# The last two tiles' squares of four norms go to TensorE

## What is computed

```
def rmsnorm(x, g):
    xf = x.astype(jnp.float32)
    y = xf * lax.rsqrt(jnp.mean(xf * xf, axis=-1, keepdims=True) + EPS)
    return y.astype(x.dtype) * g
...
    x = x + gate1 * (merged @ w_out[l])
    h2 = _rmsnorm(x, norm2_g[l]) * (1.0 + scale2) + shift2
    x = x + gate2 * _conv_ffn(h2, w_up[l], conv_w[l], conv_b[l], w_down[l])
return _rmsnorm(x, final_g)
...
    h = rmsnorm(x, g_mix)
    proj = h @ w_in
...
    x = x + merged @ w_o
    h2 = rmsnorm(x, g_ffn)
    a, b = jnp.split(h2 @ w_up, 2, axis=-1)
```

## Time and profile before

| | us |
|---|---|
| median of 3 runs | 894.43 |
| lowest, highest | 894.06, 895.6 |
| span of the profiled execution | 894.5 |
| busy in it: TensorE matmuls, VectorE, ScalarE | 853.3, 594.6, 409.9 |
| adds of this kind (L717): 35 | 0.43 us each |
| matmuls of the means by this line (L1219): 20 passes | 0.17 to 0.38 us each |

### The profile page before, as it was taken

One profiled execution on the slowest core, in us unless ns is written; L12 is line 12 of the kernel. 1 busy time (PEld: TensorE's weight loads), 2 busy tenths in 40 slices (PEclk: granted clock), 3 DMA queues, 4 the chain that ended last, 5 costly groups with the idle time before them and its releaser, 6 DMA issues.

```text
span 894.5 us, 16350 instructions
## 1 busy us (share of the span) xinstructions
PE 853.3 (95%) x6912; PEld 839.3 (94%) x6912; DVE 594.6 (66%) x789; ACT 409.9 (46%) x516; POOL 6.1 (1%) x22
## 2 busy tenths in 40 slices
PE   3499999998999999999999999999999899999998
PEld 3499899998899999999999999999999899999998
DVE  5987899477976656656774348644586766656663
ACT  3344666433544444434653345555424654434440
POOL 1100000000000000000000000000000000000000
PEclk9999999999799999999999999999999799999999
DMA  9788468537465555553265335353544455455511
GB/s 355 316 326 331 144 209 318 191 132 282 193 232 188 185 177 173 178 182 140 96 236 174 110 141 189 105 180 141 188 143 175 152 181 178 174 181 184 188 47 48
DMA packets 23676, 166.85 MB, mean 187 GB/s; under 512 B 2752, under 2 KB 3008, under 8 KB 3520
## 3 DMA queue, kind: packets, MB, share of 16 engines
q1 hardware_dynamic: 23040, 164.64, 51.2%
q10 hardware_dynamic: 576, 1.35, 0.4%
HBM read 164.93 MB, written 1.05 MB: 186 GB/s over the span
## 4 chain that ended last, share of the span: by engine, by line
PE 90%; DVE 6%; DMA 2%; issue 1%; ACT 0%; SPq 0%; DVEq 0%; ACTq 0%
PE ps L1167 78%; PE ps L1207 6%; DMA raw<-in_w_ada 2%; PE ps L1258 1%; PE ps L1245 1%; PE ps L1316 1%; DVE ada L674 1%; DVE wlo L689 1%; PE ps L1228 1%; DVE ada L678 1%; PE ps L1345 1%; PE ps L1297 1%; PE ps L1296 1%; DVE probs L828 0%; DVE tmp L754 0%
## 5 line engine op out<-in xcount | busy, mean ns | idle before, releaser
L689 DVE TENSOR_TENSOR wlo<-raw,whi 128x2048 fp32r<-128x2048 f32 x131 | 299.4, 2290 | 187.9 <-ACT whi L364 187.4
L1167 PE MATMUL ps<-hhi,whi 128*128 128x256 f32 x1368 | 392.2, 287 | 0.0
L1167 PE MATMUL ps<-hlo,whi 128*128 128x256 f32 x1368 | 387.9, 284 | 0.0
L1167 PE MATMUL ps<-hhi,wlo 128*128 128x256 f32 x1368 | 387.8, 283 | 0.0
L364 ACT ACTIVATE whi<-raw 128x2048 fp32r<-128x2048 f32 x131 | 249.9, 1910 | 176.2 <-PE ps L1167 149.6
L1167 PEld LDWEIGHTS ps<-hhi,whi 128*128 128x128 f32 x1368 | 263.1, 192 | 4.6 <-issue 4.5
L1167 PEld LDWEIGHTS ps<-hlo,whi 128*128 128x128 f32 x1368 | 263.2, 192 | 0.1
L1167 PEld LDWEIGHTS ps<-hhi,wlo 128*128 128x128 f32 x1368 | 263.0, 192 | 0.0
L1167 PE MATMUL ps<-fhi,whi 128*128 128x256 f32 x352 | 99.8, 284 | 0.3 <-DVE flo L1024 0.3
L1167 PE MATMUL ps<-fhi,wlo 128*128 128x256 f32 x352 | 99.7, 283 | 0.0
L1167 PE MATMUL ps<-flo,whi 128*128 128x256 f32 x352 | 99.7, 283 | 0.0
(11 more groups left out here) (163 smaller groups left out, 951.5 us busy)
## 6 DMA issues: line engine op xcount, KB each, us to landing
raw<-in_w_up SPq DMA_DIRECT2D x44, 1024.0 KB, 4.9
raw<-in_w_in SPq DMA_DIRECT2D x43, 1024.0 KB, 4.9
raw<-in_w_ada SPq DMA_DIRECT2D x24, 1024.0 KB, 6.2
raw<-in_w_down SPq DMA_DIRECT2D x22, 1024.0 KB, 4.9
raw<-in_branches SPq DMA_DIRECT2D x10, 1024.0 KB, 5.1
raw<-in_w_out SPq DMA_DIRECT2D x4, 1024.0 KB, 4.8
raw<-in_w_mem_kv SPq DMA_DIRECT2D x4, 1024.0 KB, 4.8
raw<-in_w_o SPq DMA_DIRECT2D x4, 1024.0 KB, 4.8
```

The costliest lines, as they stand in the source:

```text
L689: V.tensor_tensor(wlo[:, w % SPLIT, :], raw[:, r % RAW, :], f32(whi[:, w % SPLIT, :]), ALU.subtract).then_inc(raw_done, 1)
L1167: ins = mm(out_, l, r, start=start and i == 0, stop=stop and i == 2, **kw)
```

## The change

VectorE adds tiles 0 to 5 only in "two", "final", "mix" and "ffn2" (five adds instead of seven; "mem" stays as it is). TensorE's mean then has six matmuls instead of two: tile 0, which now holds the sum of tiles 0 to 5, and tiles 6 and 7 straight from ScalarE's squares, all accumulated in the same two columns of PSUM. Ahead of tile 6 TensorE waits for the norm's fourth pair of squares: `sq_ready` counts 4 for each norm, and NORM_SQUARES says how many norms came before.

```diff
--- before.py
+++ after.py
@@ -116,6 +116,7 @@
     STAT[_name] = (N_STAT, NT * (_tiles * _heads or 1))
     N_STAT += STAT[_name][1]
 SUMMED = ("mem", "two", "final", "mix", "ffn2")
+NORM_SQUARES = {"two": 2, "final": 3, "mix": 4, "ffn2": 5}
 BCAST = 256
 
 
@@ -715,7 +716,7 @@
                 for c in (2 * i, 2 * i + 1):
                     if c:
                         ins = V.tensor_tensor(src[:, 0, :], src[:, 0, :], src[:, c, :], ALU.add)
-                        if c < KT - 1:
+                        if c < (KT if name == "mem" else KT - 2) - 1:
                             link(ins)
                         else:
                             ins.then_inc(sem(f"{name}_summed"), 1)
@@ -980,7 +981,6 @@
                     sum_squares("two", 2, mg, u - 1)
                 if u in (1, 2):
                     split_low(w + AHEAD)
-            sum_squares("two", 2, mg, 3)
             norm_wide(1, "two", x, lambda c: gs2[:, c:c + 1], shift=mod[:, 24:32])
             split_low(WO1 + 3 + AHEAD)
 
@@ -1062,7 +1062,7 @@
                     ins = V.scalar_tensor_tensor(out=x[:, c, :], in0=ps[:, 4 + u, S * i:S * i + S],
                                                  scalar=mod[:, 40 + c:41 + c], in1=x[:, c, :], op0=ALU.mult, op1=ALU.add)
                 ins.then_inc(sem("x2_ready"), 1)
-            for i in range(4):
+            for i in range(3):
                 sum_squares("final", 3, mg, i)
             split_low(MEMKV + 3)
             invert("final")
@@ -1145,7 +1145,6 @@
                     sum_squares("ffn2", 5, mg, u - 1)
                 if u in (1, 2):
                     split_low(w + AHEAD)
-            sum_squares("ffn2", 5, mg, 3)
             norm_wide(4, "ffn2", x, lambda c: col("g_ffn_2", c))
             split_low(WO2 + 3 + AHEAD)
             ffn(1)
@@ -1214,9 +1213,14 @@
                 tiles, heads, bank, _ = NORMS[name]
                 mean = mean_64[:, 0:P:64] if heads == 2 else (mean_128 if heads else mean_d)[:, 0:1]
                 if name in SUMMED:
+                    parts = (0,) if name == "mem" else (0, KT - 2, KT - 1)
                     pe.wait_ge(sem(f"{name}_summed"), 1)
-                    for tt in range(NT):
-                        ins = mm(ps[:, bank, tt:tt + 1], src[:, 0, P * tt:P * tt + P], mean, start=True, stop=True)
+                    for c in parts:
+                        if c == KT - 2:
+                            pe.wait_ge(sem("sq_ready"), 4 * NORM_SQUARES[name] + 4)
+                        for tt in range(NT):
+                            ins = mm(ps[:, bank, tt:tt + 1], src[:, c, P * tt:P * tt + P], mean,
+                                     start=c == 0 and tt == 0, stop=c == parts[-1], skip_group_check=True)
                     ins.then_inc(sem(f"{name}_mean"), 1)
                     return
                 for c in range(tiles):
```

## The result

The changed kernel is slower: 899.34 us median of 5 runs (lowest 897.77) against 894.43 us; by the ratio, 1.0044 with an interval of 1.003 to 1.0057, it is +3.9 us. One of the five executions took 1052.92 us at a mean granted clock of 0.751: the ratio leaves it out, the median doesn't, and the other four have a median of 898.74 us. The forecast was 896.3 us, with a range to 898.0: the sign was right, the size too small. Its profiled execution has a span of 897.4 us and a time of 899.35 us.

What follows compares the result with a forecast made beforehand. TensorE, busy 95% of the span, was taken as the bound. Terms -0.03 ("two"), +0.90 ("final"), +0.90 - 0.2 ("mix") and +0.2 ("ffn2") sum to +1.8 us on 894.51: 896.3 us, range 894.9 to 898.0.

Steps and rivals of the forecast that it cites:

- What bounds which norm: At "two" and "ffn2" TensorE waits for VectorE's adds; at "final" and "mix" they finish 2.0 and 2.3 us early.
- "two" and "ffn2": Norms ahead of the feed-forward blocks: eight more passes against 0.92 us of adds removed, -0.03 us and +0.2 us.
- A shift of its start counts half: Weight unit behind "two": if the clock rises at the same moment as before, half the start's shift counts, giving -0.03 us.
- within 0.2 us of 3.6: Sign at "two": ScalarE's root comes within 0.2 us of 3.6 us behind TensorE's last matmul.
- so half of 0.43 comes back: -0.2: Weight unit behind "mix": starting later, it uses 2.99 us of the half-clock stretch instead of 3.42, giving -0.2 us.
- rival C: Clock rises later behind "mix", by 3.42 us, costing 1.7: 898.0 us; second form, also at another norm, 899.7; chance 0.07.
- The base: Starting figure for the sum: the profiled span of 894.51 us, taken as 0.08 us above the median of the runs.
- eight passes at half clock: Price of the passes added to a norm's mean on TensorE at 1.2 GHz: 0.213 us each, 1.71 us.
- the lower end of "two": Term at "two" with all passes at full clock: -0.02 us before halving.
- Rival A: Clock stays full through the head of one feed-forward block, 3.2 us back: 893.1 us; chance 0.07.
- a clock that stays up past 222.6: Sign at "two" said to decide for the rival that the clock is kept: no fall at 222.61 us.
- Rival B: Passes are cheap at all four norms, 0.68 us for eight instead of 0.90: +1.1, 895.6 us; chance 0.10.

Runs made afterwards that it cites:

- e4_final: The change at "final" only, against the kernel before: 895.83 us, ratio 1.0015 (1.0006 to 1.0025), +1.3 us.
- e6_mix: The change at "mix" only, against the kernel before: 895.8 us, ratio 1.001 (1.0001 to 1.0019), +0.9 us.
- e12_middle_passes: The kernel before with all seven adds, plus eight further unused TensorE passes at "final" and "mix": 896.95 us, ratio 1.0029, +2.6 us.
- e2_heads: The change at "two" and "ffn2" only, against the kernel before: 894.33 us, ratio 0.9998 (0.9989 to 1.0007), -0.2 us.
- e8_heads_passes: The kernel before with all seven adds, plus eight further unused TensorE passes at "two" and "ffn2": 897.43 us, ratio 1.003, +2.7 us.
- e1_before: The kernel before, with no edit, run again: ratio 1.000 (0.9991 to 1.0009), 11 executions of 893.67 to 895.97 us.
- e5_after: The whole change again with more executions, against the kernel before: 896.94 us, ratio 1.0033 (1.0021 to 1.0045), +3.0 us.
- e3_middle: The change at "final" and "mix" only, against the kernel before: 896.57 us, ratio 1.0025 (1.0016 to 1.0034), +2.2 us.
- e9_mix_filled: The change plus four unread 256-column matmuls in TensorE's idle time behind "mix": 897.05 us, ratio 1.0028 against the kernel before.
- e11_before_filled: The kernel before plus unread 256-column matmuls in TensorE's idle time at "two", "mix" and "ffn2": 890.24 us, ratio 0.9947, -4.7 us.

## Why the prediction was right or wrong

**What bounds which norm: right.** Two norms wait for the adds, two don't. e4_final, e6_mix and e12_middle_passes show it from three sides.

**"two" and "ffn2": right as a sum** (+0.17 forecast, -0.2 measured with e2_heads, zero within its interval), for a reason that was partly wrong. "A shift of its start counts half" rested on the clock rising at the same moment whatever the start. e8_heads_passes contradicts it: with the mean 1.5 and 0.9 us later at the heads than in e1_before its total was +2.7 us, and its profile had "two" at 16.65 us instead of 14.52 (15.74 in before). The moments at which the clock changes are not fixed to the program: it fell at 222.61 in one execution of before and in e1_before at 224.46. One of the prediction's signs missed for that reason: in the profile of after the root at "two" comes 3.28 us behind TensorE's last matmul (224.14 - 220.86), not within 0.2 us of 3.6, as the clock fell only at 225.15, behind the mean.

**The step that failed is "mix": "so half of 0.43 comes back: -0.2".** The stage was forecast at +0.90 - 0.2 = +0.7 and measured +1.95, +1.6 and +1.88 in after, e5_after and e3_middle. In place of a relief of 0.2 stands a cost of 0.7 to 1.05 us. The prediction let the clock rise at its old moment, with the unit merely missing a part of the half-clock stretch. Instead the rise moved: the next unit started 1.0 us (after), 1.8 us (e5_after) and 1.2 us (e3_middle) behind the fall of the clock, and the clock then rose 6.8 us after the fall instead of 3.4. That is rival C in its first form (C was given 0.07). In the seven profiles without both changes and without fillers the unit started ahead of the fall or 0.1 us behind it, and the stretch was 3.4 us in each. e12_middle_passes, with the same shift and no adds removed, has 6.8 again; e9_mix_filled, where the clock doesn't fall, has the stage at 10.70 us. The price per stretch was too high in C (1.7 us), because at full clock the unit is held by VectorE's tiles and by the next split, as e9_mix_filled shows.

With the measured +1.6 to +1.95 in the place of +0.7 the sum is +2.7 to +3.0 us, and e5_after has +3.0 (+1.9 to +4.1). The times alone bear the step out less firmly than the profiles: for "final" and "mix" together the forecast has +1.6 and e3_middle +2.2 (+1.4 to +3.0), and the parts of the change add up to +2.1, not far from the +1.8 forecast. About 0.25 us of the +3.0 lies outside the span: e5_after's times are on average 2.05 us above their spans, those of before 1.80.

**The base was off, too.** The sum was set on a span of 894.51 us as if it were a time. A time lies 1.8 us above the span (e1_before), and that execution's span was about 1.7 us above the mean of its kernel, 892.8 us over e1's 44 executions of it. The two errors cancelled in the number, by luck. What they hid is the scatter: the 11 executions of e1_before differ by up to 2.3 us, which five of them don't average out: the changed kernel's 898.74 us (of four) and 896.94 (of seven) lie 1.8 us apart.

Two slips of the prediction changed nothing: eight passes at half clock are 1.70 us, not 1.71, and the lower end of "two" (-0.02) lies above its middle (-0.03).

**Rival A** didn't come about in the change (the clock fell at "two" at 225.2 and rose near 232.0 in the profile of after), though its sign, a clock that stays up past 222.6, came about. That sign tells nothing: e1_before, without the change, kept the clock until 224.46. But the mechanism is real: e11_before_filled gains 4.7 us by nothing else. Its price, 3.2 us per head, is what the table has against the profile it was read from (15.74 against 12.68 at "two", 15.27 against 12.08 at "ffn2"); against e1_before it is 1.8 and 2.2 us. **Rival B** falls with the price of a pass.

**Left open:** in how many executions the longer stretch occurs. It was there in all four profiles with both norms' passes, but e3_middle's median is +2.2 us, less than its profile's stages add up to (2.8), so it is probably not in all. An estimate from each execution's span and mean granted clock, 2 x (1 - clock) x span, has 26.3 us at half clock on average in before. Against before on the same chip "final" alone adds 0.7 us of it, "mix" alone 0.8, both 2.0 and the whole change 2.7; a stretch of 6.8 us in place of 3.4 in every execution would add 3.4. Also open is why the change's time lies 1.9 to 2.1 us above its span instead of 1.8.

## What to carry to other kernels

Moving work from an idle engine to the one that bounds pays only where the second is waiting for it: look at each place separately, and split such a change. Two of these four norms broke even and two cost their full price. Where the bounding engine has idle gaps of 2 to 3 us, what it does in them can be worth more than the work that the change is about: here fillers in the gaps of three norms gave 4.7 us, an earlier sum 1.6, and both 5.3. And before a forecast of a few tenths of a per cent, find out how far one profiled execution is from the middle of its kernel.

## What was not expected of the hardware

Four to eight matmuls of 256 float32 columns in TensorE's gaps at a norm kept the granted clock at 2.4 GHz through it, where it had fallen with gaps of 0.5 and 1.8 us around the broadcast; the granted clock of the whole execution rose from 0.985 to 0.994. How long half clock lasted went with when the next weight unit started, in all of 63 stretches: 3.4 us where it started ahead of the fall or up to 0.46 us behind it, 6.8 us at 0.94 to 3.61 us, 10.2 us from 4.17 us on. So a start that is later by under a microsecond can cost another 3.4 us at half clock. And two executions of one program had these stretches at different matmuls, with spans from 891.9 to 894.2 us in e1_before.
